# Sample states pass through one buffer in the retention heads; each strip's load waits for the preceding strip's store

## What is computed

```python
def step(r, qkv):
    qc, kc, vc = qkv
    s = jnp.einsum('bihd,bjhd->bhij', qf, kf) * intra[None]
    o = jnp.einsum('bhij,bjhe->bihe', s, vf)
    o = o + jnp.einsum('bihd,bhde->bihe', qf, r) * q_dec
    r = r * c_dec + jnp.einsum('bjhd,bjhe->bhde', kf * k_dec, vf)
    return r, o
```

## Time and profile before

| | us |
|---|---|
| median of 3 runs | 1750.88 |
| lowest, highest | 1749.67, 1751.84 |
| the profiled execution's own time | 1747.55 |
| its span, first to last instruction | 1745.7 |
| TensorE busy in the span | 1696.8 (97%) |
| VectorE, ScalarE, GpSimd busy | 751.1, 564.1, 382.8 |
| four retention heads, about | 487 to 892 |
| mean granted TensorE clock | 0.999 |

### The profile page before, as it was taken

How to read it: one execution, slowest core, us unless ns; L and a number is a source line. 1 busy time by engine, 2 the same in 40 slices (tenths; PEclk the granted TensorE clock), 3 DMA queues, 4 the chain that set the end, 5 groups by cost and what they waited for, 6 DMA issues and landing times.

```text
span 1745.7 us, 22335 instructions
## 1 busy us (share of the span) xinstructions
PE 1696.8 (97%) x8585; PEld 1341.8 (77%) x8585; DVE 751.1 (43%) x1561; ACT 564.1 (32%) x926; POOL 382.8 (22%) x501
## 2 busy tenths in 40 slices
PE   3999999999999999999999999999999999999998
PEld 2899998777876667667678888888788877778876
DVE  4664442212244545545543334745553016444432
ACT  4311121111134434444431224425222135444442
POOL 2111112111133334342322225314200000110000
PEclk9999999999999999999999999999999999999999
DMA  9544545553466667677662211332323635432201
GB/s 310 177 150 172 186 142 200 182 205 137 156 212 180 218 210 235 187 231 239 219 231 68 90 49 37 120 104 80 101 84 98 206 125 191 131 104 73 73 25 37
DMA packets 137002, 260.73 MB, mean 149 GB/s; under 512 B 16931, under 2 KB 60095, under 8 KB 136898
## 3 DMA queue, kind: packets, MB, share of 16 engines
q1 hardware_dynamic: 104114, 167.23, 30.0%
q0 software_dynamic: 32784, 92.08, 15.5%
HBM read 178.83 MB, written 80.43 MB: 149 GB/s over the span
## 4 chain that ended last, share of the span: by engine, by line
PE 86%; DVE 4%; DMA 2%; issue 2%; ACT 2%; POOL 0%; SPq 0%; DVEq 0%; POOLq 0%
PE trunk_ps L1111 35%; PE in_ps_o L535 12%; PE in_ps_o L531 11%; PE tail_ps L1989 6%; PE tail_ps L1980 4%; PE tail_ps L1947 3%; PE trunk_ps L1154 3%; PE trunk_ps L1138 2%; PE tail_ps L1957 2%; DVE room L1544 1%; PE trunk_ps L1215 1%; PE in_ps_o L556 1%; PE tail_ps L1923 1%; PE trunk_ps L1149 1%; DMA out_state_prompt<-room 1%
## 5 line engine op out<-in xcount | busy, mean ns | idle before, releaser
L1111 PE MATMUL trunk_ps<-w_hi,hT_hi 128*128 128x512 f32 x1008 | 410.3, 407 | 0.0
L1111 PE MATMUL trunk_ps<-w_hi,hT_lo 128*128 128x512 f32 x1008 | 401.0, 398 | 0.0
L1111 PE MATMUL trunk_ps<-w_lo,hT_hi 128*128 128x512 f32 x1008 | 397.3, 394 | 0.0
L1111 PEld LDWEIGHTS trunk_ps<-w_hi,hT_hi 128*128 128x128 f32 x1008 | 189.3, 188 | 59.0 <-issue 17.5
L1111 PEld LDWEIGHTS trunk_ps<-w_lo,hT_hi 128*128 128x128 f32 x1008 | 189.5, 188 | 49.7 <-issue 5.0
L1111 PEld LDWEIGHTS trunk_ps<-w_hi,hT_lo 128*128 128x128 f32 x1008 | 189.2, 188 | 44.4
L208 DVE TENSOR_TENSOR w_lo<-w_raw,w_hi 128x1024 fp32r<-128x1024 f32 x76 | 96.5, 1271 | 115.1 <-ACT w_hi L196 109.7
L531 PE MATMUL in_ps_o<-hT_hi,w_hi 128*128 128x384 f32 x384 | 130.6, 340 | 0.4 <-DVE hT_lo L662 0.4
L531 PE MATMUL in_ps_o<-hT_hi,w_lo 128*128 128x384 f32 x384 | 129.1, 336 | 0.0
L531 PE MATMUL in_ps_o<-hT_lo,w_hi 128*128 128x384 f32 x384 | 129.1, 336 | 0.0
L535 PE MATMUL in_ps_o<-w_hi,hT_hi 128*128 128x512 f32 x288 | 114.4, 397 | 0.0
(11 more groups left out here) (243 smaller groups left out, 2811.5 us busy)
## 6 DMA issues: line engine op xcount, KB each, us to landing
w_raw<-in_a_w_in SPq DMA_DIRECT2D x96, 256.0 KB, 3.4
room<-in_state_ret SPq DMA_DIRECT2D x64, 256.0 KB, 4.1
out_state_sample<-room POOLq DMA_DIRECT2D x64, 256.0 KB, 6.8
room<-in_b_ada_w SPq DMA_DIRECT2D x24, 512.0 KB, 6.7
scratch_qkT<-room POOLq DMA_DIRECT2D x48, 192.0 KB, 2.2
scratch_v_hi<-room POOLq DMA_DIRECT2D x36, 256.0 KB, 2.6
scratch_v_lo<-room POOLq DMA_DIRECT2D x36, 256.0 KB, 3.1
scratch_o<-room POOLq DMA_DIRECT2D x36, 256.0 KB, 3.3
```

Of the source, the lines that this page charges most:

```text
L1111: ins = pe.matmul(ps[:, bank, :], h[:, k, t * P:(t + 1) * P], w[:, (C0 + j) % 2, k, :], start=k + m == 0, stop=k == KT - 1 and m == 2)
```

## The change

`r` has one place of four tiles, in the second half of the old room. `load_r(k)` waits for the store of strip k - 1, with the two counters kept in turn. The second load ahead of the heads is gone. Within a head the loads are issued at t = 0 (strip 0, from head 1 on), and at t = 3, 5 and 7 (strips 1, 2 and 3). In SyncE's code the new line stands behind the weight piece of t = 3 and ahead of those of t = 5 and 7. TensorE, VectorE and GpSimd use the one place; their order is as before.

```diff
--- before.py
+++ after.py
@@ -766,7 +766,7 @@
         rows = at(11776, 2, D)
         z = at(13824, KT, P)
 
-        r = at(0, 2, 4, DV)
+        r = at(2048, 4, DV)
         part = lambda o, n: pr.parts[:, o:o + n]
         v_hi, v_lo = (part(o, 2 * DV).rearrange("p (a b) -> p a b", a=2) for o in (0, 2 * DV))
         k_hi, k_lo = part(4 * DV, DK), part(4 * DV + DK, DK)
@@ -942,10 +942,10 @@
                 if k == 0:
                     for sem_, count in pr.intake_stored:
                         sp.wait_ge(sem_, count)
-                if k >= 2:
-                    sp.wait_ge(r_stored[k % 2], 64 * (k // 2))
+                if k:
+                    sp.wait_ge(r_stored[(k - 1) % 2], 64 * ((k - 1) // 2 + 1))
                 for j in range(4):
-                    sp.dma_start(r[:, k % 2, j], dr["state_ret"][2 * j + par, h, a * P:(a + 1) * P, :]).then_inc(r_in[k % 2], 16)
+                    sp.dma_start(r[:, j], dr["state_ret"][2 * j + par, h, a * P:(a + 1) * P, :]).then_inc(r_in[k % 2], 16)
 
             def load_weights(c, i):
 
@@ -1027,7 +1027,6 @@
             load_r(0)
             load_weights(1, 1)
             load_qk(1)
-            load_r(1)
             for h in range(RH):
                 for t in range(T):
                     if h == RH - 1 and t + 1 < T:
@@ -1038,8 +1037,10 @@
                         load_qk(3 * h + 2)
                     if t == 3:
                         load_weights(h + 1, 3)
-                    if t in (2, 4, 6, 8) and 4 * h + t // 2 - 1 + 2 < 4 * RH:
-                        load_r(4 * h + t // 2 - 1 + 2)
+                    if t == 0 and h:
+                        load_r(4 * h)
+                    if t in (3, 5, 7):
+                        load_r(4 * h + t // 2)
                     if t == 4 and h == RH - 2:
                         for half in range(2):
                             sp.wait_ge(o_stored[half], 16 * T)
@@ -1169,7 +1170,7 @@
                 pe.wait_ge(r_in[i % 2], 64 * (i // 2 + 1))
                 pe.wait_ge(qs_ready, h + 1)
                 for j in range(4):
-                    ins = pe.matmul(ps[BR * j:BR * (j + 1), PS_STR, :], qs[:, par, a, BR * j:BR * (j + 1)], r[:, i % 2, j, :],
+                    ins = pe.matmul(ps[BR * j:BR * (j + 1), PS_STR, :], qs[:, par, a, BR * j:BR * (j + 1)], r[:, j, :],
                                     start=False, stop=q == 3, tile_position=(0, BR * j), skip_group_check=True)
                 ins.then_inc(o_done if q == 3 else s_ready, 1)
                 pe.wait_ge(decayed, score_no(h, min(2 * q + 2, 7)) + 1)
@@ -1454,7 +1455,7 @@
                         par, a = strip_tile(t) // 2, strip_tile(t) % 2
                         pool.wait_ge(strip_new, 4 * i + 4)
                         for j in range(4):
-                            pool.dma_start(dr["state_sample"][2 * j + par, h, a * P:(a + 1) * P, :], r[:, i % 2, j]).then_inc(r_stored[i % 2], 16)
+                            pool.dma_start(dr["state_sample"][2 * j + par, h, a * P:(a + 1) * P, :], r[:, j]).then_inc(r_stored[i % 2], 16)
                     if t == SELF:
                         pool.wait_ge(state_new, PT * h + PT)
                         pool.dma_start(dr["state_prompt"][h].rearrange("(a p) c -> p a c", p=P), state[:, :, :]).then_inc(p_stored, 16)
@@ -1541,7 +1542,7 @@
                 dve.wait_ge(strips_done, i + 1)
                 dve.wait_ge(*((o_done, T * h + T) if q == 3 else (s_ready, 3 * h + q + 1)))
                 for j, bank in STRIP:
-                    dve.scalar_tensor_tensor(r[:, i % 2, j], r[:, i % 2, j], GAMMA[h] ** DEC_SEQ, ps[:, bank, :], ALU.mult, ALU.add).then_inc(strip_new, 1)
+                    dve.scalar_tensor_tensor(r[:, j], r[:, j], GAMMA[h] ** DEC_SEQ, ps[:, bank, :], ALU.mult, ALU.add).then_inc(strip_new, 1)
 
             def statistics(h, t):
```

## The result

The changed kernel took 1824.59 us (median of 4 runs, 1822.25 to 1830.04) against 1751.36 us of the kernel before (4 runs): a ratio of 1.0427, 95% interval 1.0411 to 1.0442, 73 us more. Predicted were 1818 us and a range of 1788 to 1842. The profiled execution is the slowest of the four, 1830.04 us with a span of 1828.2; beside the kernel before's 1747.55 and 1745.7 that is 82.5 us more.

The account below looks back on a forecast made before the run. TensorE was taken to bound the kernel, with state loads wholly hidden. 52.5 + 7.0 + 4.5 + 6.8 - 3.6 = 67.2 us on 1747.55 gave 1814.8 profiled, 1818 us as median, range 1788 to 1842.

Parts of the forecast that it names:

- part 2: Strip 1's load, behind the weight piece waiting for VectorE's split, stalls TensorE once per head: 52.5 us (41 to 59).
- part 1: One buffer, each load waiting for the preceding store: strip 3 late in heads 0 to 2, 4.5 us (0 to 9).
- part 4: Head 3: loads of strips 2 and 3 behind the o rows, each late by 3.5 us, together 7.0 (5 to 9).
- part 5: TensorE's clock falls after each of four long stalls, 1.7 us lost each: 6.8 us; nothing for five short stalls.
- part 3: After each strip 1 stall VectorE is idle and ready, so 0.9 us return: 3.6 us in all (0 to 6).
- Bound: Claim that matmul work is 86% of the span, so whatever stops TensorE goes straight into the time.
- the 10 us that the prediction had named as a sign of being wrong: Forecast would be wrong if landings behind the weight load took 5 or 10 us; it took 8.4.
- The row at 720: State load behind much traffic in the kernel before, 9.9 us to last landing, taken as the high end for strip 1.
- The Trainium skill's estimate of the prediction: By its DMA fit, v, weights and states issued from 536.5 land 6.8 us later; stall 10.5 us, total 11 us lower.
- (a): Rival: only the store counts, the split being over before strip 1's load could go; some 16 us, 1767 us; 7%.
- (b): Rival: not slower, strip 1's loads being in before TensorE's read because the weight load is not blocked; 1751 us; 4%.
- (c): Rival: longer chains, strip 2 also late in heads 0 to 2, clock low twice as long; about 1850 us; 11%.

Follow-up runs that it names:

- order_only: Changed kernel with two buffers and the old store waits (load k waits for store k-2), loads still issued where the change puts them: 1819.99 us.
- ahead_of_weights: Changed kernel, still one buffer, with the state load of t == 3 moved ahead of the weight piece: 1775.13 us.
- gate_then_state: Changed kernel; at t == 3 SyncE waits for the same split, then issues the state load first and the weight piece behind it: 1817.32 us.
- ahead_of_all: As ahead_of_weights, with a head's three state loads at the top of the tile, ahead of head 3's loads of o rows: 1763.14 us.
- filled: Changed kernel with 48 matmuls, results never read, put before TensorE's wait for strip 1 in each head: 1818.85 us.
- again: The changed kernel without an edit, timed once more beside the next runs on the same chip: 1826.64 us.
- v_behind_state: Changed kernel; at t == 3 GpSimd waits until strip 1 has landed before issuing that tile's two v loads: 1814.46 us.
- state_alone: As gate_then_state, with SyncE also waiting until the state has landed before it issues the weight piece: 1814.41 us.

## Why the prediction was right

It was right in sign and mechanism, and the time lies within its range. The size is in part luck. Profiled execution against profiled execution it was 15.3 us short (67.2 for 82.5); two terms, parts 5 and 3, were mis-sized against each other, and the median missed by only 6.6 us, as the profiled execution of before was faster than its four timed runs beside the changed kernel, and that of the changed kernel the slowest of four. By its own steps, in us of the profiled execution:

| step | predicted | measured |
|---|---|---|
| part 2, strip 1 behind the weight piece, 4 waits | 52.5 | 57.1 |
| part 1, strip 3 of heads 0 to 2 | 4.5 | 6.8 |
| part 4, head 3's strips 2 and 3 | 7.0 | 5.9 |
| part 5, clock (measured: half of the work at 0.50, an estimate) | 6.8 | 19.6 |
| part 3, given back (measured: the remainder) | -3.6 | -10.0 |
| in the heads | 67.2 | 79.4 |
| ahead of the first strip | 0 | 3.1 |

**Bound.** That TensorE had no cover of its own for a late state held; 69.7 us of waits stand in the 79.4 us by which the heads are longer.

**Part 2** held in its cause, shown from both sides (order_only keeps it with two buffers, ahead_of_weights takes away all but 8.8 of its 57.1 us with one). The gate itself was sized right: in head 0 the state load is issued 4.7 us after the reader stands, for 4.8 predicted. The term was 4.6 us short, and the failing piece is the time from first issue to last landing: 8.4 us taken, 9.8, 9.6, 10.6 and 8.4 measured; the third passes the 10 us that the prediction had named as a sign of being wrong. More than half of that is the issue: behind the weight piece the last of the four DMAs starts 2.0, 2.6, 2.2 and 1.6 us after the first, not 1.3; in gate_then_state, with the weights behind, it is 1.4 again. The rest may be order: at 526 and 572 the first state DMA was issued ahead of the v loads (526.30 against 526.43, 572.69 against 573.00), here all four behind them (540.65 against 539.54 and 540.07). The row at 720, 9.9 us, came nearest by its number, but the order there was that of 526, so it was no better ground. The Trainium skill's estimate of the prediction (page "DMA: Bandwidth & Descriptors", section "Anatomy of one DMA — SWDGE (gpsimd) path"), 6.8 us from 536.5 on, was further off: the same data took 550.43 - 539.54 = 10.9 us.

**Part 1** held: waits of 2.6, 1.6 and 2.6 us before strip 3 for 2.4, 1.3 and 0.8, no wait before strip 0, and order_only removes just these. The reason given for strip 3's slower load does not hold: in the trace of before the next part's weights had landed by 569 us and the qkT loads by 573.5; what was issued beside the load of 572.69 were GpSimd's store of o and its two v loads, from 572.40 to 573.53. That these slow it too, as at strip 1, was not tried. The cost of one buffer is bound to the rest, though: with the order mended it is 13.6 us and not 6.6.

**Part 4** held: 3.1 and 2.8 us for 3.5 each, gone in ahead_of_all.

**Part 5** is the term that was mis-sized, by a factor of three. The fall came four times of four, as said. But it had taken the low stretch from the earlier trace rows, 3.4 us at 0.50, half lost; behind the long idles TensorE worked 5.1 to 6.3 us at 0.50, so 11.6 us are lost and not 6.8. And the short stalls, counted at nothing, had a low stretch too in four of five cases (3.4, 3.4, 3.2 and 6.0 us of work, 8.0 lost). The step that was wrong is the count of nothing for them, together with the one short row for the length. "filled" shows that this costs time, and at the rate assumed: in the heads TensorE worked 36.8 us at 0.50 in "again" and 22.0 in "filled", by the records of the clock; half the difference is 7.4 us. The two profiled executions are 10.1 us apart (7.8 by the medians), and the short waits that shrank make 3.0 of them, so some 7 are left for the clock. The Trainium skill, page "TensorE: Matmul & The Clock Gate", section "HAM oscillation — how this bites in real kernels", tells of waits for a DMA between bursts of matmuls that let the clock fall every time. The trace agrees for the four long waits, four of four, and nearly so for the five short ones, four of five, though the waits of that section are longer than these.

**Part 3** erred the other way. From strip 1 to strip 2 of a head some 1.1 to 1.4 us return, as said (25.28 us for 23.28 in head 0, of them 3.2 for the clock, leaves 22.1). But the same happens behind the stalls of strip 3 and of head 3's strip 2: less the low clock, the interval to the next strip is 0.6 to 1.2 us shorter than before, four times of four. For about half of the 10.0 us the trace names VectorE: TensorE's listed waits for it in the heads are 5.4 us before, 2.7 of them in the earlier trace rows, and 0.8 after. The 10.0 itself is what is left of the sum, not measured, and what makes the other half is not shown.

**Ahead of the first strip** the profiled execution is 3.1 us later than that of before: its clock is at 0.50 up to 41.4 us, where before it was full from 38.2 on, and once more at 495 us for 3.4 us. The code up to there is the same but for one load less. Two things speak for spread and not for the change: v_behind_state, with the same load less, has the full clock at 495 us and reads its first strip 1.2 us earlier than the changed kernel; and the kernel before spreads over 7 us in its own runs (1746.5 to 1753.4), with mean granted clocks of 0.992 to 1.0. It is also a part of the difference between the 82.5 us of the profiles and the 73 us of the medians.

**The rivals.** (a), that only the store counts, is what ahead_of_weights built: 1775 us, for the 1767 given, which lacked head 3's first strip and the clock, and put strip 1 of head 1 at 0 where the rows of before give 1.2 us (load issued at 623.36, landed 8.4 us later, reader at 630.55); it measured 0.7. (b) did not occur: the weight piece was issued right behind the split in all four heads, and the state load behind it. (c) did not occur in its chain: strip 2 of heads 0 to 2 had 7.6 to 8.1 us to spare in the changed kernel, since behind a stall the store lands 5 us after its first issue and not 8. Its other half, a clock low for twice as long, came true and more: 19.6 us are lost by it, for 6.8 in the forecast and 7 on top in (c).

## What to carry to other kernels

A load's start is decided by what stands ahead of it on its issuing queue, not only by its own wait: before a buffer is given up, write down for each load the latest wait of any instruction ahead of it and compare it with the reader. Here one line's place cost 51 us, the place of head 3's loads behind the o rows 12, and the buffer itself 14. If a buffer is to be given up, hand it over in the pieces in which it is stored; that brought the old time back with half the room. And count a stall of the matmul engine with its clock: behind each idle of 13 to 15 us it ran 5 to 6 us at half speed.

## What was not expected of the hardware

- **Short idles and the clock.** In the changed kernel idles of 2.6 to 3.1 us, in a stretch otherwise full of matmuls, were followed by 3.2 to 6.0 us of work at 0.50; one of 1.57 us was not. But the length alone doesn't decide: in "again" an idle of 2.95 us and in "filled" one of 3.11 left the clock full, and in ahead_of_weights one of 1.73 didn't. Before, 1.9 us at 492 had left it full, and so did the same idle of 2.1 us in v_behind_state; in the changed kernel and in "again" it was followed by 3.4 us at 0.50. Of the waits of 9 us or more in all the traces, 28 of 28 were followed by a low clock. So runs of one kernel differ by their clock: of the five of ahead_of_all, the one at 1754.9 us has a mean of 0.998, the four at 1760.4 to 1763.7 have 0.989 to 0.995.
- **Loads issued by GpSimd right behind its store.** While the first 3 us of the two v loads ran, issued 0.6 and 1.1 us after the store of o, the engines moved 91 GB/s at a share of 0.84, and a state load from the other queue was held back: landing up to 7.7 us after issue with them, 3.9 without. Issued when the state was in, the same v loads caused no such stretch: from 546 to 549 us, with the weights beside them, the engines moved 315 GB/s. Whether it's the store ahead of them or the read itself was not tried.
- **Weights beside a state load.** 0.5 MB ahead, behind, or absent changed the time from first issue to last landing by under 1 us on average while the v loads were there (9.5, 8.8 and 8.5 us over the four heads of "again", gate_then_state and state_alone), and by 0.2 to 2.1 us, head by head, when they were not.
